# Tiles 36 to 61 in the wide form, split pairs, gathers respaced, and folds placed before the last splits

## The reference

```
s[t, h, c, :]  = (x @ wq)[t, h, c] . sub_keys[h, c]       8 heads, 2 halves, 128 keys
expert[t, h*16+k], gate = the 16 best sums of both halves, softmax over them
a[t, e]  = gelu(down[expert[t, e]] . x[t])
out[t]   = sum over e of a[t, e] * gate[t, e] * up[expert[t, e]]
```

## Time and profile before

| what | us |
|---|---|
| timed runs, median of 3 | 1041.38 (1039.97 to 1044.31) |
| the profiled execution | 1037.82 |
| its span, first to last instruction | 1036.0 |
| TensorE busy in the span | 1009.8 (97%) |
| VectorE busy | 799.9 (77%) |
| ScalarE busy | 534.9 (52%) |
| POOL busy | 233.4 (23%) |

### The profile page before, as it was taken

The page is one execution under the profiler, slowest core; times in us unless marked ns, Lnnn a source line. Parts: engine busy times, 40 slices in busy tenths (PEclk is TensorE's granted clock), DMA queues, the critical chain, the costliest instruction groups (busy, mean ns, idle before and its releaser), DMA issues.

```text
span 1036.0 us, 20304 instructions
## 1 busy us (share of the span) xinstructions
PE 1009.8 (97%) x8228; PEld 949.7 (92%) x8228; DVE 799.9 (77%) x1380; ACT 534.9 (52%) x883; POOL 233.4 (23%) x231
## 2 busy tenths in 40 slices
PE   9999999999999999989999999999999999999967
PEld 8987888898799999989999999999999999999954
DVE  5667766846679999767999889677777878787764
ACT  5554545454365455566655555544444445554450
POOL 3000000100068894622222211010010122223200
PEclk9999999999999999999999999999999999999989
DMA  9943334642446567888888887677777788998931
GB/s 323 383 158 102 103 102 160 234 138 82 150 135 202 191 206 218 286 313 285 286 283 290 285 263 267 220 230 232 228 227 233 227 314 312 302 335 307 336 126 41
DMA packets 67261, 236.05 MB, mean 228 GB/s; under 512 B 9184, under 2 KB 9744, under 8 KB 66784
## 3 DMA queue, kind: packets, MB, share of 16 engines
q1 hardware_dynamic: 49536, 178.28, 51.7%
q0 software_dynamic: 17056, 55.94, 15.9%
q10 hardware_dynamic: 576, 0.52, 0.2%
HBM read 224.72 MB, written 8.39 MB: 225 GB/s over the span
## 4 chain that ended last, share of the span: by engine, by line
PE 89%; DMA 6%; DVE 2%; ACT 1%; issue 1%; SPq 0%; ACTq 0%
PE psG L1589 16%; PE psG L1591 15%; PE psG L1590 15%; PE psS L1990 5%; PE psG L1990 4%; PE psT L1990 4%; DMA raw<-in_up 3%; PE psO L1591 3%; PE psO L1589 3%; PE psO L1590 3%; PE psS L1991 2%; PE psG L1991 2%; PE psT L1991 2%; DMA raw<-in_down 2%; PE psO L1946 1%; PE psO L1947 1%
## 5 line engine op out<-in xcount | busy, mean ns | idle before, releaser
L797 ACT ACTIVATE hi<-raw 128x1024 fp32r<-128x1024 f32 x325 | 343.6, 1059 | 316.0 <-DMA raw<-in_up 168.0
L1049 DVE TENSOR_TENSOR lo<-raw,hi 128x1024 fp32r<-128x1024 f32 x291 | 353.5, 1219 | 81.0 <-ACT hi L797 80.2
L1589 PE MATMUL psG<-b_two,hi 128*128 128x224 f32 (+1 forms) x1088 | 302.9, 278 | 4.3 <-ACT H L991 3.9
L1591 PE MATMUL psG<-b_two,lo 128*128 128x224 f32 (+1 forms) x1088 | 299.1, 275 | 0.0
L1590 PE MATMUL psG<-b_two,hi 128*128 128x224 f32 (+1 forms) x1088 | 299.1, 275 | 0.0
L1589 PEld LDWEIGHTS psG<-b_two,hi 128*128 128x128 f32 x1088 | 208.7, 192 | 6.7 <-issue 3.8
L1590 PEld LDWEIGHTS psG<-b_two,hi 128*128 128x128 f32 x1088 | 208.8, 192 | 0.1
L1591 PEld LDWEIGHTS psG<-b_two,lo 128*128 128x128 f32 x1088 | 208.8, 192 | 0.0
L727 POOL TENSOR_TENSOR lo<-raw,hi 128x1024 fp32r<-128x1024 f32 x34 | 82.3, 2432 | 102.6 <-ACT hi L797 102.3
L1567 DVE TENSOR_TENSOR act_two<-H,act_two 128x224 fp32r<-128x224 f32 x128 | 49.2, 387 | 67.4 <-ACT act_two L1028 67.0
L1990 PE MATMUL psS<-act_two,hi 128*128 128x448 f32 x240 | 85.7, 387 | 2.2 <-DVE lo L1049 1.7
(11 more groups left out here) (367 smaller groups left out, 2050.0 us busy)
## 6 DMA issues: line engine op xcount, KB each, us to landing
raw<-in_down SPq DMA_DIRECT2D x128, 512.0 KB, 4.5
raw<-in_up SPq DMA_DIRECT2D x128, 512.0 KB, 4.5
raw<-in_w_stream SPq DMA_DIRECT2D x73, 512.0 KB, 3.8
one_kept<-one POOLq DMA_DIRECT2D x28, 256.0 KB, 4.6
one<-one_kept POOLq DMA_DIRECT2D x28, 256.0 KB, 4.3
w<-in_w SPq DMA_DIRECT2D x4, 512.0 KB, 12.4
xT<-in_xT SPq DMA_DIRECT2D x4, 256.0 KB, 5.6
memT<-in_memT SPq DMA_DIRECT2D x1, 1024.0 KB, 7.2
```

The lines of the kernel that those rows point to most:

```text
L797: act.activation(hi[hi_slot(n)][:], raw[slot(n)][:], ACT.Copy).then_inc(hi_done, 1)
L1049: dve.tensor_tensor(lo[slot(n)][:], raw[slot(n)][:], hi[hi_slot(n)][:].bitcast(FP32), ALU.subtract)\
L1589: pe.matmul(out, hi_l, hi_r, start=start, stop=False)
L1591: return pe.matmul(out, lo_l, hi_r, start=False, stop=stop)
```

## The change

Down tiles 36 to 61 take the wide form. The 32 gathers of down rows are spread evenly over slots 42 to 119 (before: every second slot from 42 to 72, every third from 74 to 119). The 32 steps that add up rows start at slot 8 instead of 62: ten of them at 8, 13, ..., 53, the other 22 from 58 to 115 (before: 62 to 116, four steps in seven slots). Each gather's wait moves with it, five slots ahead. The activation of two up tiles is split by one operation of each engine, in four pair buffers. The high part of the pair j+3, j+4 is placed at odd slots j, behind the split of tile j+4, and waits for tile j to be used. The splits of late tiles: 120 and 121 behind slot 116, 122 and 123 behind slot 117, each two now on their own and not inside the up step; 124 to 126 behind the folds and behind the pair 122/123. The pairs 124/125 and 126/127 and the split of 127 stand behind slot 120, where the four single activations stood. Tiles 118 and 119 are computed together, chunk by chunk: TensorE waits for the low parts of both, then does chunk 0 of 118, chunk 0 of 119, chunk 1 of 118, and so on. `raised_x` and one buffer of the one-hot matrices move in SBUF.

```diff
-WIDE = []
-APART_AT = [42 + 2 * k for k in range(SPAN)] + [74 + 3 * k for k in range(SPAN)]
+WIDE = list(range(36, 62))
+APART_AT = [42 + 77 * q // (APART - 1) for q in range(APART)]
 COEF_AT = [APART_AT[SPAN * i + SPAN - 1] + 4 for i in range(SETS)]
-RAISE_AT = [62 + 7 * q // 4 for q in range(APART)]
+RAISE_AT = [8 + 5 * q for q in range(10)] + [58 + 57 * q // 21 for q in range(APART - 10)]
...
-        if j + 4 < E_TILES - 4:
-            out.append(("act", j + 4))
+        if j % 2 and j + 3 < FOLDED + 2:
+            out.append(("act", (j + 3) // 2))
+        if j in (FOLDED - DEPTH, FOLDED - DEPTH + 1):
+            first = FOLDED + 2 * (j - FOLDED + DEPTH)
+            out += [("late", first), ("late", first + 1)]
         if j == FOLDED - 1:
-            out += [("fold", c) for c in range(KD)]
+            out += [("fold", c) for c in range(KD)] + [("act", FOLDED // 2 + 1)]
+            out += [("late", m) for m in range(FOLDED + 4, E_TILES - 1)]
         if j == E_TILES - LAST:
-            out += [("act", E_TILES - 4 + i) for i in range(4)] + [("late", E_TILES - 1)]
+            out += [("act", E_TILES // 2 - 2), ("act", E_TILES // 2 - 1), ("late", E_TILES - 1)]
...
-                    if 4 <= j < E_TILES - 4:
-                        act.wait_ge(tile_used, UP + j - 3)
-                    act.activation(act_two[act_slot(j)][:, 0, :], H[:, j, :], ACT.Copy).then_inc(act_hi, 1)
+                    if 2 <= j < E_TILES // 2 - 2:
+                        act.wait_ge(tile_used, UP + 2 * j - 2)
+                    act.activation(act_pair[pair_slot(j)][:, :, 0, :], H[:, 2 * j:2 * j + 2, :], ACT.Copy).then_inc(act_hi, 1)
...
-                elif what == "up":
-                    for late in late_tiles(j):
-                        split(UP + late)
...
+                    two = act_pair[pair_slot(j)]
+                    dve.tensor_tensor(two[:, :, 1, :], H[:, 2 * j:2 * j + 2, :], two[:, :, 0, :].bitcast(FP32), ALU.subtract)\
...
+            def up(tiles):
+                for j in tiles:
+                    lo_wait(UP + j)
+                    pe.wait_ge(act_lo, j // 2 + 1)
+                    if j == 0:
+                        pe.wait_ge(h_out, E_TILES)
                 for c in range(KD):
+                    for j in tiles:
+                        up_chunk(j, c)
...
-                elif what == "up":
-                    up(j)
+                elif what == "up" and j < FOLDED - 2:
+                    up((j,))
+                elif what == "up" and j == FOLDED - 1:
+                    up((j - 1, j))
```

More of the change, by code:

```diff
@@ L267, in slot, with pair_slot @@
     return (n - N1 + N1 % EARLY - (EARLY - RING if n >= UP + E_TILES - LAST else 0)) % RING
-def act_slot(j):
-    return j % 4 + (4 if j >= E_TILES - 4 else 0)
+def pair_slot(p):
+    return p % 2 + (2 if p >= E_TILES // 2 - 2 else 0)
 def slots():
@@ L341, in table_order @@
         if j == E_TILES - 3:
-            out += [("act", 0), ("act", 1)]
-    out += [("act", 2), ("act", 3)]
+            out.append(("act", 0))
+    out.append(("act", 1))
     for j in range(E_TILES):
@@ L363 @@
 TABLE_ORDER = table_order()
-def late_tiles(j):
-    first = E_TILES - LAST + 2 * (j + DEPTH - (E_TILES - LAST))
-    return range(max(first, E_TILES - LAST), min(first + 2, E_TILES - 1))
 class Steps:
@@ L461, in build @@
         same1 = sb("same1", [P, TOK // 2, HALF, 2], F16)
-        one1 = [sb(f"one1_{i}", [P, 2, TOK // 2, HALF, 2], F16) for i in range(2)]
+        one1 = [sb(f"one1_{i}", [P, 2, TOK // 2, HALF, 2], F16, at=(None, late_at)[i]) for i in range(2)]
         one1_hi, one1_lo = ([one1[i][:, c] for i in range(2)] for c in range(2))
         act_at = place["at"]
-        place["at"] += 2 * SD * 4
+        place["at"] += 4 * SD * 4
         expert = sb("expert", [P, SETS, TOPK], U32)
@@ L471, in build @@
         of_token = sb("of_token", [P, 3 * SPAN])
-        raised_x = [sb(f"raised_x{i}", [P, D], at=R_at + (36 + 4 * i) * 1024) for i in range(SETS)]
+        raised_x = [sb(f"raised_x{i}", [P, D], at=at) for i, at in enumerate((B_at + 8192 + 4 * SD * 4, R_at + 36 * 1024))]
         turned_x = sb("turned_x", [P, KD, SD], at=R_at + 48 * 1024)
@@ L477, in build @@
         ln_last = sb("ln_last", [P, 2, D], at=B_at)
-        act_two = [sb(f"act_two{i}", [P, 2, SD], F32R, at=at)
-                   for i, at in enumerate((late_at, act_at, B_at + 8192, B_at + 8192 + 2 * SD * 4))]
+        act_pair = [sb(f"act_pair{i}", [P, 2, 2, SD], F32R, at=at) for i, at in enumerate((act_at, B_at + 8192))]
         place["at"] = R_at + (EARLY - RING) * 4096
         hi_last = [sb(f"hi_last{i}", [P, D], F32R) for i in range(DEPTH)]
-        for i in range(4, 8):
-            act_two.append(sb(f"act_two{i}", [P, 2, SD], F32R))
+        for i in range(2, 4):
+            act_pair.append(sb(f"act_pair{i}", [P, 2, 2, SD], F32R))
         H_REUSED = -(-(place["at"] - R_at) // (SD * 4))
@@ L629, in build, with act_two @@
         block = ctx.enter_context(nc.Block())
+        def act_two(j):
+            return act_pair[pair_slot(j // 2)][:, j % 2]
         def chunk_bank(c):
@@ L675, in _ @@
                 if n == UP + E_TILES - LAST:
-                    sp.wait_ge(act_lo, RAW_REUSED)
+                    sp.wait_ge(act_lo, (RAW_REUSED + 1) // 2)
                 src = a["w_stream"][n] if n < DOWN else a["down"][n - DOWN] if n < UP else a["up"][(n - UP) * P:(n - UP + 1) * P]
@@ L793, in split @@
                 if n == UP + E_TILES - LAST:
-                    act.wait_ge(act_lo, H_REUSED)
+                    act.wait_ge(act_lo, (H_REUSED + 1) // 2)
                 if HI_BEFORE[n] is not None:
@@ L1001, in _ @@
                     if j == 0:
-                        act.wait_ge(act_lo, TURNED_H)
+                        act.wait_ge(act_lo, (TURNED_H + 1) // 2)
                     act.wait_ge(chunk_done, j + 1)
@@ L1023, in _ @@
                         act.wait_ge(gated, GROUPS)
-                    if j == HALF:
+                    if j == HALF // 2:
                         act.wait_ge(gated, 2 * GROUPS)
-                    if 4 <= j < E_TILES - 4:
-                        act.wait_ge(tile_used, UP + j - 3)
-                    act.activation(act_two[act_slot(j)][:, 0, :], H[:, j, :], ACT.Copy).then_inc(act_hi, 1)
+                    if 2 <= j < E_TILES // 2 - 2:
+                        act.wait_ge(tile_used, UP + 2 * j - 2)
+                    act.activation(act_pair[pair_slot(j)][:, :, 0, :], H[:, 2 * j:2 * j + 2, :], ACT.Copy).then_inc(act_hi, 1)
                 elif what == "up" and j + DEPTH < E_TILES - LAST:
                     split(UP + j + DEPTH)
-                elif what == "up":
-                    for late in late_tiles(j):
-                        split(UP + late)
                 elif what == "late":
@@ L1538, in _ @@
                         rest(UP + j + 3)
-                    if j + DEPTH >= E_TILES - LAST:
-                        for late in late_tiles(j):
-                            rest(UP + late)
                 elif what == "late":
@@ L1566, in _ @@
                     dve.wait_ge(act_hi, j + 1)
-                    dve.tensor_tensor(act_two[act_slot(j)][:, 1, :], H[:, j, :], act_two[act_slot(j)][:, 0, :].bitcast(FP32), ALU.subtract)\
+                    two = act_pair[pair_slot(j)]
+                    dve.tensor_tensor(two[:, :, 1, :], H[:, 2 * j:2 * j + 2, :], two[:, :, 0, :].bitcast(FP32), ALU.subtract)\
                         .then_inc(act_lo, 1)
@@ L1965, in last @@
                             n = UP + j
-                            s, q = hi_slot(n), act_slot(j)
+                            s, two = hi_slot(n), act_two(j)
                             lo_wait(n)
-                            pe.wait_ge(act_lo, j + 1)
+                            pe.wait_ge(act_lo, j // 2 + 1)
                             for left, right, st in ((0, hi[s], j == j0), (0, lo[slot(n)], False), (1, hi[s], False)):
                                 for c in columns:
-                                    pe.matmul((psS, psT)[t][0:width, c * 512:(c + 1) * 512], act_two[q][:, left, cut],
+                                    pe.matmul((psS, psT)[t][0:width, c * 512:(c + 1) * 512], two[:, left, cut],
                                               right[:, c * 512:(c + 1) * 512], start=st, stop=False)
@@ L1978, in last, with up_chunk @@
                         mm.then_inc(first_half if t == 0 else third_quarter if columns == (0,) else tile_used, 1)
[L1980 to L1986, removed]
-                for c in range(KD):
[L1988 to L1997, removed]
+            def up_chunk(j, c):
+                n, s, two = UP + j, hi_slot(UP + j), act_two(j)
+                out, cut, st = chunk_bank(c), slice(c * P, (c + 1) * P), j == 0 and c < KD - 1
+                if c < WIDE_CHUNKS:
+                    pe.matmul(out[:, 0:2 * SD], hi[s][:, cut], two.rearrange("p a n -> p (a n)"), start=st, stop=False)
```

(17 more changed lines are left out.)

## The result

The changed kernel takes 1046.76 us in the median of 13 runs (1043.07 to 1054.6), the kernel before 1040.54 in 13 runs. The ratio is 1.0068 with a 95% interval of 1.0049 to 1.0087: 7.1 us slower by the ratio (6.2 by the medians), where 10 us faster was forecast and 1040 was the upper end of the range. The profiled execution is the slowest of the 13, 1054.6 us, so its trace shows the losses larger than the median has them.

What follows compares the result with a forecast made beforehand. TensorE, busy through the long stretches, was taken to bound the kernel, with a 7 us hole before `last`. End 8.0 + wide tiles and gathers 2.5 - pairs 0.5 = 10.0 us faster: 1031 us from 1041.38, range 1023 to 1040.

Steps and rivals of the forecast that it cites:

- The wide tiles: Down tiles 36 to 61: one fewer matmul per set saves 4.8 us, but waits for VectorE's sum take part of it.
- the first rival: Down tiles 36 to 61: late landings make the wide loop bind and pairs lose 4 us; 1049 in all, chance 0.07.
- I take 2.65 from tile 45 on: Wide down tiles from 45 on: 2.65 us per tile, against a mean of 2.83 before.
- The pair of stretch and gathers: Tiles 36 to 61, wide form and even gathers together: 2.5 us gained, bounds -6 and +7.
- The pace of the matmuls: Wide down tiles: sets of two matmuls 0.3125 us apart, against 0.336 for sets of three; 4.8 us saved.
- The pairs: Up phase, one activation operation for two tiles: a loss of 0.5 us, bounds -1 (a gain) and 8.
- L + 2.35: Up phase: the pair's chain from the end of tile j-1, L being the transfer's landing time; three tiles cover L to 5.35.
- The second rival: Second half of the up phase: pairs bind at L = 6, 57 tiles lose 9 us, half likelier; 1040, chance 0.14.
- The end: Last tiles, folds ahead of late splits: the 7 us hole shrinks to about one; 8.0 us gained, bounds 4 and 9.
- T0 + 26.2: When the first-half pass of `last` ended before, T0 being the end of up tile 117; forecast after: T0 + 18.1.
- clock term: First 48 matmuls of `last`: 12.79 us before, 11.3 at full clock; the slow start costs 1.5.
- The gathers: Tiles 36 to 61: gathers no longer pile up, so some 2 of 3 us of stalls go.

Runs made afterwards that it cites:

- e10: Kernel before with wide tiles 36 to 61 alone, two banks, old gathers; 1050.35 us, ratio 1.0091.
- e1: Changed kernel with the list of wide down tiles empty, all else as changed; 1038.41 us, 0.9981 of the kernel before.
- e4: Changed kernel with down tiles from 36 on cycling over four PSUM banks instead of two; 1034.69 us, 0.9941 of the kernel before.
- e13: Kernel before with new end, even gathers, single activations, four banks from tile 36, wide tiles 46 to 61; 1026.68 us, ratio 0.9865.
- e15: Kernel before with new end, even gathers, single activations, four banks from tile 36, no wide tile; 1031.11 us, ratio 0.9911.
- e2: Kernel before with even gathers and new end, single activations, no wide tile; 1032.78 us, ratio 0.9935.
- e5: e1 with the pair's high part moved ahead of the split of tile j+4; 1034.65 us, 0.9953 of the kernel before.
- e3: Kernel before with the new end alone; 1034.96 us, ratio 0.9946.
- e12: Kernel before with the even gathers alone; 1042.46 us, ratio 1.0012.

## Why the prediction was wrong, step by step

**The wide tiles, the step that failed.** The loop was written down as it is: tile j behind the sum of j-2, behind the low part, behind a high part, behind a transfer; and the first rival, slower, named it with a chance of 0.07. It tied the loss to landings of 6.1 us and more, though, and in e10, which lost 9.5 us, the median landing from 400 to 474 was 4.6. What failed is the price: "two stalls of 1 to 2.4 us, so about 2 us are lost there" for tiles 36 to 44, and "I take 2.65 from tile 45 on". The trace has four waits of 2.2, 1.1, 3.3 and 1.6 us in the first ten tiles, 8.1 together, and those tiles took 11.8 us longer than before. The 16 behind took 44.5 us, 2.8 each: there the gain was 2.1 us, against some 3 in the working. Two things were left out. The sum stands behind everything VectorE has in the slot ahead, and for the sum of tile 42, for which tile 44 waits, that is the last decode, the gate weights and a product in a row, 3.9 us (420.65 to 424.58) and not 2.4. And the clock, 4.6 us in the first ten tiles and 1.6 behind tile 63, stood nowhere in the sum. The pair of stretch and gathers was put at 2.5 us gained; e1 and e10 show 9.0 and 9.5 lost by the wide tiles alone. That the cause is the wait for a sum only two tiles back, and not the wide matmuls or the added copies and sums, is shown by e4, which keeps all of these and stands 4 us under e1.

The pace of the matmuls was right: sets 0.313 apart in wide tiles at full clock (396.36 to 401.06), against 0.336. By the 6 + columns cycles of the Trainium skill ("VectorE: DVE Perf Modes", the section on the TRN2 errata) three and two matmuls would take the same 0.29 us, an estimate; the trace agrees for neither. Whether this gain ever reaches the end is what e13 and e15 leave open.

**The pairs.** Mis-sized: 0.5 forecast, 4.8 measured (e1 less e2). The chain was right, three tiles against L + 2.35, and e5 confirms its place. The bound of L = 5.35 was held against a median: in e1 the median landing from 860 to 984 was 4.5, well inside it, and 5.4 us of waits came all the same. The second rival's 4.5 to 9 us were nearer in size, though its landings of 6 were not seen. In the chain of waits of the changed kernel the late ones stand one by one:

```profile
905.48 6.40 DMA raw<-in_up
922.16 6.33 DMA raw<-in_up
938.77 6.57 DMA raw<-in_up
986.39 8.53 DMA raw<-in_up
```

The last gave the wait of 3.22 us shown above, with a granted clock of 0.73 and 0.84 in the eight us from 996.

**The end.** Right in mechanism, 5.6 us (e3) against 8.0, inside its bounds of 4 and 9. (Its T0 + 26.2 is 26.3 by its own terms, which changes nothing.) The missing part is waits ahead of tiles 118 and 119 and on the first fold (1.1 + 1.4 + 1.4 in e3, 1.4 forecast). Its clock term, 1.5 us, came nearly as forecast: 12.79 to 11.42 is 1.4.

**The gathers.** They were to return some 2 of the 3 us of waits on H; in e12 the waits on H between 285 and 984 are 6.6 us, in the kernel before 4.4. Fewer gathers at a time do lower the traffic from 840 to 984, from 317 GB/s to 284 in e12 and 271 in the changed kernel (280 forecast), but no time comes of it alone. The 1.1 us by e2 less e3 can't be told from none.

**The sum of the measured parts** is 9.0 + 4.8 - 5.6 - 1.1 = 7.1 us. It is exact because each run is the base of the next, so it proves nothing by itself; that e10, in another order, gives 9.5 for the same 9.0 is in keeping with parts that hardly act on each other.

## What to carry to other kernels

Before an edit that saves matmul time by one more step on another engine, count how many tiles may pass before that step's result is wanted, and hold this against the worst slot of that engine's list and the latest transfers, not against means and medians. If it is one tile, buy slack first: two more PSUM banks, idle in that phase, took away all of the 9 us (e4 is 4 us under e1, and the banks alone, without wide tiles, are worth 2.5 to 4.4). An operation for two tiles takes on the lateness of the second one: place it by what it needs, ahead of the neighbour that waits for a transfer.

## What was not expected of the hardware

Behind one wait of 2.17 us the granted clock was at its lower level (mean 0.58 from 404 to 408, sets 0.59 instead of 0.31 apart) and came back only while TensorE worked on; in the kernel before the stretch with a wait of 1.7 us shows 1.00 throughout. So the price of such a wait was 2.17 us and 1.7 more. The length of the wait alone doesn't decide it: the wait of 1.68 us at 484.53 in the changed kernel was followed by 0.73 and 0.84 (shown above), one of 1.74 in e4, at 402.95, by 1.00. What does is not shown.

The changed kernel spreads over 11.5 us, from 1043.07 to 1054.6, the one before over 6.1 in those 13 runs, but over 8.8 in the 25 of another job, and e5, which has no wide tile, over 11.6: the spread is not the wide tiles' alone. The mean clock was 0.995 in the fastest run of the changed kernel and 0.990 in the slowest. That is about 5 us by estimate, so the clock makes at most about half of this spread; where the rest comes from is open.
